# The prologue of a pooling and sparse-attention decoder step: quarters, group by group, keys by halves, and half of the key rows issued by GpSimd

## The reference

```python
hn = _rmsnorm(h, norms_l[0])
ext = concatenate([buf, hn], axis=1)              # buf: 15 older normed inputs (zeros for the prompt)
# group g of 512 channels: mean over the last w = 2, 4, 8 or 16 positions, less the input itself
s = c[:, POOL_BUF+1 : POOL_BUF+1+S] - c[:, POOL_BUF+1-w : POOL_BUF+1-w+S]      # c: running sum of ext
cnt = jnp.minimum(w, pos + 1)
mix = s / cnt - xf[:, POOL_BUF:]
mix = einsum('bsgc,gcd->bsgd', mix, w_pool_l) * scale_l       # a 512 x 512 matrix for each group
h = h + _rmsnorm(mix, norms_l[1]);  then a SwiGLU feed-forward of width 5632
# _compress of the past rows of each sample, keys and values (c = 0, 1), 16 pages of 128 rows each
first  = einsum('bnjche,cjef->bnchf', sub + pe[:16], cmp_w1[:, :16])
second = einsum('bnjche,cjef->bnchf', sub + pe[16:], cmp_w1[:, 16:])
hid = gelu(first[:, :-1] + second[:, 1:] + cmp_b1);  out = hid @ cmp_w2
```

## Time and profile before

| | us |
|---|---|
| median of three runs (range) | 2597.3 (2594.82 to 2601.64) |
| profiled execution, its own time | 2593.98 |
| span of the profile | 2592.4 |
| TensorE busy | 2528.8 (98%) |
| VectorE, ScalarE, GpSimd busy | 1212.3, 912.9, 291.1 |
| mean granted TensorE clock | 0.994 |

### The profile page before, as it was taken

How to read it: one execution, slowest core, us unless ns; L and a number is a source line. 1 busy time by engine, 2 the same in 40 slices (tenths; PEclk the granted TensorE clock), 3 DMA queues, 4 the chain that set the end, 5 groups by cost and what they waited for, 6 DMA issues and landing times.

```text
span 2592.4 us, 44035 instructions
## 1 busy us (share of the span) xinstructions
PE 2528.8 (98%) x17340; PEld 2476.0 (96%) x17340; DVE 1212.3 (47%) x1372; ACT 912.9 (35%) x1130; POOL 291.1 (11%) x324
## 2 busy tenths in 40 slices
PE   8799999999999999999999999999999999999997
PEld 6699999999999999999998789899999999999997
DVE  6654444444444444553434744744444444444444
ACT  3354323323332333442324643633333223323332
POOL 2430000000000001310001321300000000000012
PEclk9899999999999999999999999999999999999999
DMA  6524444444444444445545455344444444344443
GB/s 254 179 98 146 152 162 149 151 149 158 149 154 157 155 146 156 136 154 175 163 154 202 164 167 171 114 146 152 156 160 146 154 154 154 136 162 160 148 152 128
DMA packets 88809, 403.36 MB, mean 156 GB/s; under 512 B 13244, under 2 KB 23884, under 8 KB 58930
## 3 DMA queue, kind: packets, MB, share of 16 engines
q1 hardware_dynamic: 78674, 382.72, 43.5%
q0 software_dynamic: 6160, 12.60, 1.5%
q10 hardware_dynamic: 3920, 7.34, 0.8%
HBM read 394.88 MB, written 19.02 MB: 160 GB/s over the span
## 4 chain that ended last, share of the span: by engine, by line
PE 87%; DVE 6%; ACT 3%; issue 1%; SPq 1%; POOL 1%; DMA 1%; DVEq 0%; ACTq 0%
PE ps L1296 27%; PE ps L1297 27%; PE ps L1298 27%; ACT w_hi L479 1%; DVE w_lo L751 1%; PE ps L1387 1%; PE ps L1548 1%; PE ps L1474 1%; DVE winB L858 1%; DVE winA L858 1%; ACT y L587 0%; ACT x_hi L505 0%; SPq L361 0%; PE ps L1545 0%; POOL sc L1261 0%
## 5 line engine op out<-in xcount | busy, mean ns | idle before, releaser
L1296 PE MATMUL ps<-x_hi,w_hi 128*128 128x320 f32 x3536 | 1094.8, 310 | 5.9 <-DVE sg L922 2.4
L1297 PE MATMUL ps<-x_lo,w_hi 128*128 128x320 f32 x3536 | 1092.9, 309 | 0.0
L1298 PE MATMUL ps<-x_hi,w_lo 128*128 128x320 f32 x3536 | 1092.9, 309 | 0.0
L751 DVE TENSOR_TENSOR w_lo<-w_raw,w_hi 128x2048 fp32r<-128x2048 f32 (+1 forms) x364 | 748.9, 2058 | 651.8 <-ACT w_hi L479 651.8
L479 ACT CAST w_hi<-w_raw 128x2048 fp32r<-128x2048 f32 (+1 forms) x364 | 623.0, 1712 | 532.3 <-PE ps L1298 477.7
L1296 PEld LDWEIGHTS ps<-x_hi,w_hi 128*128 128x128 f32 x3536 | 664.1, 188 | 8.1 <-DVE sg L922 3.0
L1297 PEld LDWEIGHTS ps<-x_lo,w_hi 128*128 128x128 f32 x3536 | 664.0, 188 | 0.4 <-issue 0.2
L1298 PEld LDWEIGHTS ps<-x_hi,w_lo 128*128 128x128 f32 x3536 | 664.0, 188 | 0.0
L1296 PE MATMUL ps<-hid_hi,w_hi 128*128 128x320 f32 x1408 | 435.1, 309 | 0.0
L1297 PE MATMUL ps<-hid_lo,w_hi 128*128 128x320 f32 x1408 | 435.1, 309 | 0.0
L1298 PE MATMUL ps<-hid_hi,w_lo 128*128 128x320 f32 x1408 | 435.1, 309 | 0.0
(11 more groups left out here) (234 smaller groups left out, 1509.7 us busy)
## 6 DMA issues: line engine op xcount, KB each, us to landing
w_raw<-w_in_dram SPq DMA_DIRECT2D x176, 1024.0 KB, 4.9
w_raw<-w_out_dram SPq DMA_DIRECT2D x128, 704.0 KB, 4.0
w_raw<-w_kv_dram SPq DMA_DIRECT2D x24, 1024.0 KB, 6.6
w_raw<-w_q_dram SPq DMA_DIRECT2D x17, 1024.0 KB, 4.9
w_raw<-w_o_dram SPq DMA_DIRECT2D x15, 1024.0 KB, 5.6
win_out_dram<-win_kv_dram POOLq DMA_DIRECT2D x8, 992.0 KB, 5.3
rowsK<-cmp_data_dram SPq DMA_DIRECT2D x16, 256.0 KB, 9.1
w_raw<-w_pool_dram SPq DMA_DIRECT2D x4, 1024.0 KB, 6.4
```

What stands on the lines that cost most here:

```text
L751: V.tensor_tensor(w_lo[:, slot, 0:width], src, w_hi[:, slot, 0:width].bitcast(F32), ALU.subtract).then_inc(lo_made, 1)
L1296: M(out, wh, xh[:, k, :], start=(k == 0), stop=False)
L1297: M(out, wh, xl[:, k, :], start=False, stop=False)
L1298: last = M(out, wl, xh[:, k, :], start=False, stop=(k == kt - 1))
```

## The change

- The square sums of x leave TensorE: x comes in quarters; ScalarE squares quarters 0 and 2, VectorE quarters 1 and 3, and VectorE adds them up to one tile, over which TensorE sums once (`x_sum`).
- `inputs(g)` and `window_sums(g)` alternate group by group, with the outgoing states copied by group. The adds skip positions that no sum needs and treat prompt and samples in two instructions; the product with the counts is done for the first w - 1 positions only, and the rest is folded into the subtraction as a constant factor.
- Key rows: pages 0 to 7 go through SyncE's queue to the lo slots' memory, pages 8 to 15 are issued by GpSimd from its own queue to the raw slots' memory. `w1K` comes in two parts and lies over y. The key compression of the first half goes in two pieces, and signals `cmp_half`.
- `w_pool[0]` and `w_pool[1]` go through `w_rawX`, over x_hi and x_lo. Their splits stand between the window sums.
- The state outputs are issued after all four groups, before the third `x_lo`. ScalarE takes pool tiles 0 to 7 out of PSUM, VectorE 8 to 15.
- Both biases become products with the weights loaded and one moving column. The value bias now stands between the pool tiles and the value compression; the second copy of `w1V` and the transposing products are gone. 20 value positions stand ahead of `acc_sum`, and 44 behind it.
- SyncE issues `w_pool[3]` before `mix_made`, and the first two feed-forward panels after eight value pages.

```diff
...
+    rowsK = (at("rowsK0", "LO", [P, NP_ALL // 2, CS, 32], off=0), at("rowsK1", "RAW", [P, NP_ALL // 2, CS, 32], off=0))
+    w1K = at("w1K", "Y", [P, CB, P], off=0)
+    sq_all = at("sq_all", "X", [P, 4, GC * NT], off=0)
+    w_rawX = at("w_rawX", "X", [P, PW], off=KT // 2 * NT * 4)
...
+    winA = at("winA", "Z", [P, GC, EXT], off=0)
     winB = at("winB", "Z", [P, GC, EXT])
+    inv = at("inv", "Z", [P, NG, CS])
...
+        for i in range(4):
+            sp.dma_start(h[:, i * GC:(i + 1) * GC, :], x[:, i * GC:(i + 1) * GC, :]).then_inc(x_in[i], 16)
...
-        sp.dma_start(w1K[:, :, :], cmp_w1[0]).then_inc(cmpK_in[0], 16)
+        sp.dma_start(w1K[:, 0:CS, :], cmp_w1[0, :, 0:CS, :]).then_inc(w1K_in[0], 16)
         sp.wait_ge(pages_in, 16)
...
+        half = NP_ALL // 2
+        for p in range(half):
+            sp.dma_start(rowsK[0][:, p, :, :], cmp_data[0, page(p)]).then_inc(cmpK_in[0], 16)
+        sp.dma_start(stS[:, :, :, :], st[:, :, :, :]).then_inc(st_in, 16)
+        sp.dma_start(w1K[:, CS:CB, :], cmp_w1[0, :, CS:CB, :]).then_inc(w1K_in[1], 16)
+        sp.dma_start(inv[:, :, :], consts[:, C_INV:C_RV].rearrange("p (g t) -> p g t", g=NG)[:, :, 0:CS]).then_inc(inv_in, 16)
+        sp.wait_ge(stat_made, 1)
+        sp.dma_start(w_rawX[:, :], w_pool[0]).then_inc(raw_in[0], 16)
...
+        sp.wait_ge(lo_made, 1)
+        sp.dma_start(w_rawX[:, :], w_pool[1]).then_inc(raw_in[1], 16)
...
         sp.wait_ge(cmp_sum, 1)
-        panel(0, 0, w_pool[0], PW)
-        panel(1, 0, w_pool[1], PW)
+        panel(2, 0, w_pool[2], PW)
+        panel(3, 0, w_pool[3], PW)
         sp.wait_ge(mix_made, NG)
         sp.dma_start(w1V[:, :, :], cmp_w1[1]).then_inc(w1V_in, 16)
-        panel(2, 0, w_pool[2], PW)
         sp.wait_ge(mix_ready, NG)
         sp.wait_ge(states_out, 32)
         for p in range(NP_ALL):
...
+            if p == half:
+                across(P_FFN0, w_in0, 0)
+                across(P_FFN0, w_in0, 1)
+            sp.dma_start(rowsV[:, p, :, :], cmp_data[1, page(p)]).then_inc(cmpV_in[p // half], 16)
+        ffn(P_FFN0, w_in0, w_out0, 2)
+        for s in range(GC):
...
+        for q in (0, 2):
+            act.wait_ge(x_in[q], 16)
+            nc.scalar.square(sq_all[:, q, :], h[:, q * GC:(q + 1) * GC, :].rearrange("p c t -> p (c t)")).then_inc(sqx_made, 1)
...
+        def save_states(g):
+            c = slice(g * GC, (g + 1) * GC)
+            act.wait_ge(ext_made, g + 1)
+            nc.scalar.copy(stP[:, c, :], ext[:, c, SEQ:EXT_P])
+            nc.scalar.copy(stS[:, c, :, :], ext_s[:, c, :, DS:EXT_B]).then_inc(ext_saved, 1)
+        def mix_high(g):
             act.wait_ge(mix_made, g + 1)
             for dst, src in zip(by_tokens(x_hi, g), by_positions(ext, g)):
                 last = nc.scalar.copy(dst, src)
             last.then_inc(mixhi_made, 1)
+        def pool_tile(n):
+            act.wait_ge(tile_made, n + 1)
+            A(y[:, n, :], ps[:, n % 2, 0:NT], ACT.Copy, scale=gn[:, G_POOL, n:n + 1]).then_inc(bank_read[n % 2], 1)
+        save_states(0)
+        mix_high(0)
+        save_states(1)
+        hi_split(0, 0, src=w_rawX[:, :])
+        mix_high(1)
+        save_states(2)
+        hi_split(1, 0, src=w_rawX[:, :])
+        act.wait_ge(lo_made, 2)
+        mix_high(2)
+        pool_tile(0)
+        pool_tile(1)
+        save_states(3)
+        pool_tile(2)
+        pool_tile(3)
+        hi_split(2, 0)
+        for n in range(GC, 2 * GC - 1):
+            pool_tile(n)
+        mix_high(3)
+        pool_tile(2 * GC - 1)
+        hi_split(3, 0)
         def pool_ready(i):
...
+            if i == 12:
+                hi_split(P_FFN0, 0)
             act.wait_ge(bank_read[i % 2], i // 2 + 1)
         squares(1, y, pool_ready)
+        gelu(0, 0, hcS[:, 0, :])
+        sqrt_table()
...
+        for q in (1, 3):
+            dve.wait_ge(x_in[q], 16)
+            hq = h[:, q * GC:(q + 1) * GC, :].rearrange("p c t -> p (c t)")
+            link(V.tensor_tensor(sq_all[:, q, :], hq, hq, ALU.mult))
+            dve.wait_ge(sqx_made, q // 2 + 1)
+            link(V.tensor_tensor(sq_all[:, q - 1, :], sq_all[:, q - 1, :], sq_all[:, q, :], ALU.add))
+        link(V.tensor_tensor(sq_all[:, 1, :], sq_all[:, 0, :], sq_all[:, 2, :], ALU.add))
+        link(V.tensor_tensor(sq_all[:, 3, 0:2 * NT], sq_all[:, 1, 0:2 * NT], sq_all[:, 1, 2 * NT:4 * NT], ALU.add))
+        V.tensor_tensor(acc[:, :], sq_all[:, 3, 0:NT], sq_all[:, 3, NT:2 * NT], ALU.add).then_inc(x_sum, 1)
...
         def window_sums(g):
...
+            w = 2 ** (g + 1)
+            src, bufs = ext[:, g * GC:(g + 1) * GC, :], (winA, winB)
+            if g == 0:
+                dve.wait_ge(st_set, 1)
+                dve.wait_ge(inv_in, 16)
+            else:
                 dve.wait_ge(mix_made, g)
             for n in range(g + 1):
...
+                d, dst = 2 ** n, bufs[n % 2]
+                lo = BUF - (w - 2 * d)
+                (sp_, ss_), (dp_, ds_) = blocks(src), blocks(dst)
+                V.tensor_tensor(dp_[:, :, lo:EXT_P], sp_[:, :, lo:EXT_P], sp_[:, :, lo - d:EXT_P - d], ALU.add)
+                link(V.tensor_tensor(ds_[:, :, :, lo:EXT_B], ss_[:, :, :, lo:EXT_B], ss_[:, :, :, lo - d:EXT_B - d], ALU.add))
+                src = dst
+            (total, total_s), (x_, x_s) = by_positions(src, g), by_positions(ext, g)
+            first = total[:, :, 0:w - 1]
+            V.scalar_tensor_tensor(out=first, in0=first, scalar=float(w), in1=rep(inv[:, g, 0:w - 1], GC),
+                                   op0=ALU.mult, op1=ALU.mult)
+            full = rep(inv[:, g, CS - 1:CS].broadcast_to([P, DB * DS]), GC).rearrange("p c (b j) -> p c b j", b=DB)
+            link(V.tensor_tensor(total_s, total_s, full, ALU.mult))
+            dve.wait_ge(ext_saved, g + 1)
+            V.scalar_tensor_tensor(out=x_, in0=total, scalar=1.0 / w, in1=x_, op0=ALU.mult, op1=ALU.subtract)
+            V.tensor_tensor(x_s, total_s, x_s, ALU.subtract).then_inc(mix_made, 1)
...
+        inputs(0)
+        window_sums(0)
+        inputs(1)
+        window_sums(1)
+        dve.wait_ge(cmp_half, 1)
+        lo_split(0, 0, src=w_rawX[:, :])
+        inputs(2)
+        window_sums(2)
+        lo_split(1, 0, src=w_rawX[:, :])
+        inputs(3)
+        window_sums(3)
+        lo_split(2, 0)
+        for n in range(2 * GC, KT):
+            dve.wait_ge(tile_made, n + 1)
+            V.tensor_scalar(y[:, n, :], ps[:, n % 2, 0:NT], gn[:, G_POOL, n:n + 1], None,
+                            ALU.mult).then_inc(bank_read[n % 2], 1)
+            if n % GC == 0:
+                lo_split(n // GC + 1, 0)
+        def hidden_bias(c, col):
+            dve.wait_ge(b1_sum, c + 1)
+            V.tensor_tensor(b1e[:, c:c + 1], b1[:, c:c + 1], col, ALU.add).then_inc(b1_made, 1)
+        dve.wait_ge(const_in, 16 * 5)
+        hidden_bias(0, ps[:, 4, 0:1])
         cmp_join(0, 2, DB * NKV, True)
...
+        hidden_bias(1, ps[:, 0, 0:1])
+        dve.wait_ge(b1_made, 2)
...
+        half = NP_ALL // 2
+        pool.wait_ge(pages_in, 16)
+        for p in range(half):
+            n = pool.value_load(pgs[0:1, half + p:half + p + 1], min_val=0, max_val=cmp_data.shape[1] - 1)
+            pool.dma_start(rowsK[1][:, p, :, :], cmp_data[0, n]).then_inc(cmpK_in[1], 16)
         for g in range(NG):
             if g == 2:
+                pool.wait_ge(ext_saved, NG)
+                pool.dma_start(pool_p_out[:, :, :], stP[:, :, :]).then_inc(states_out, 16)
+                pool.dma_start(pool_s_out[:, :, :, :], stS[:, :, :, :]).then_inc(states_out, 16)
                 pool.wait_ge(states_out, 32)
...
+        def pos_bias(out, c, w1, lo, hi):
+            for j in range(lo, hi):
+                last = M(out, w1[:, j, :], pos[:, c, j:j + 1], start=(j == 0), stop=(j == CB - 1))
             return last
         pe.wait_ge(set_made, 1)
...
+        pe.wait_ge(w1K_in[0], 16)
+        pos_bias(ps[:, 4, 0:1], 0, w1K, 0, CS)
+        pe.wait_ge(x_sum, 1)
+        M(ps[:, STAT, 0:NT], ones[:, :], acc[:, :], start=True, stop=True).then_inc(stat_made, 1)
+        pe.wait_ge(cmpK_in[0], 16 * (NP_ALL // 2))
+        for j in range(CS):
+            compress(2, w1K, rowsK[0], 0, j)
+        pe.wait_ge(w1K_in[1], 16)
+        pos_bias(ps[:, 4, 0:1], 0, w1K, CS, CB).then_inc(b1_sum, 1)
+        for j in range(CS, CB):
+            last = compress(2, w1K, rowsK[0], 0, j)
+        last.then_inc(cmp_half, 1)
+        pe.wait_ge(cmpK_in[1], 16 * (NP_ALL // 2))
+        for j in range(CB):
+            last = compress(2, w1K, rowsK[1], 1, j)
         last.then_inc(cmp_sum, 1)
...
+        pe.wait_ge(w1V_in, 16)
+        pe.wait_ge(bank_read[0], KT // 2)
+        pos_bias(ps[:, 0, 0:1], 1, w1V, 0, CB).then_inc(b1_sum, 1)
+        def values(half, lo, hi):
+            n = NP_ALL // 2
+            pe.wait_ge(cmpV_in[half], 16 * n)
+            for j in range(lo, hi):
+                last = compress(5, w1V, rowsV[:, half * n:(half + 1) * n, :, :], half, j)
+            return last
```

(40 more changed lines are left out.)

136 lines of the change are left out of this document (27 added, 109 removed).

## The result

The kernel after takes 2604.5 us (median of 8 runs, 2598.0 to 2610.7), the kernel before 2596.0 (8 runs, 2594.5 to 2601.6). The ratio is 1.0032, 95% interval 1.0023 to 1.0042: 8.5 us slower, just over the 0.3% (7.8 us) that the prediction set for a difference. The forecast was 2596, in a range of 2588 to 2603, and "no change". The profiled execution took 2608.72, its span is 2607.1.

The account below looks back on a forecast made before the run. TensorE, busy 98% of the span, bounds the kernel; only the first feed-forward group's start moves. Panel split gains 10.2, value bias costs 7.1, clock 2.2: 0.9 us earlier, 2593.1 profiled, 2596 against all runs, range 2588 to 2603.

Parts of the forecast that it names:

- `inv` at 28.8: At the start, DMA engines full: `inv` lands at 28.8 us behind GpSimd's pages, and the first window sum starts at 29.
- r at 24: Root and reciprocal of x's square sums ready at about 24 us, against 23.8 before; not deciding, since `inv` is later.
- VectorE's stretch of 44.9: VectorE's window sums, inputs, splits and contention with `x_lo` take 44.9 us, so the last group is mixed at 73.9.
- `cmp_half` at 41: TensorE finishes the first half of the key compression at 41.1 us at full clock; `lo_split(0)` wants it at about 43.
- Rival B: Key compression by halves stays at 1.2 GHz, `cmp_half` comes at 58.6: 14.7 us slower, 2611; chance 0.09.
- rival C: Front of the kernel: lock contention, slower strided adds and `x_lo` of 6.5 make it 5 us late, 2600; chance 0.11.
- `x_lo` of 5.8: GpSimd's `x_lo` of the last group, beside one split, takes 5.8 us; ready at 81.1, against 81.62.
- What TensorE pays: Before the first feed-forward group: 7.1 us for the value bias now on the path, 2.2 us for the clock.
- the text's 4.4 us at half speed: After TensorE's idle time ahead of the last pool tile, some 4.4 us run at half speed: 2.2 us lost.
- 7.1 at half clock is 14: Upper bound for the value bias between pool tiles and value compression: 14 us at half clock, against the 7.1 taken.
- The forecast's own sign: Start of the first feed-forward group: net 0.9 us earlier, from 10.2 gained less 7.1 and 2.2.
- A: Rival: GpSimd's pages don't delay `inv` and the value bias costs 1.8 us: 11.5 us earlier, 2585; chance in full 0.15.

Follow-up runs that it names:

- e4: Kernel after with the second eight key pages issued by SyncE behind `inv`, none by GpSimd: 2597.8 us, 1.0007 of the kernel before.
- e6: Kernel after with TensorE's sum of squares first and the whole key bias behind the key compression: 2605.7 us, 1.0031 of the kernel before.
- e3: Kernel after with one of the 32 positions in the value bias, 31 products left out: 2588.9 us, 0.9973 of the kernel before.
- e8: Kernel before with only SyncE's order changed, `w_pool[3]` ahead of the value pages, first feed-forward panels after eight: 2591.5 us, ratio 0.9985.
- e1: Kernel after with the value bias moved ahead of the last pool tile, where TensorE idles: 2591.3 us, 0.9979 of the kernel before.
- e9: Kernel after with the value bias ahead of the last pool tile and all key rows issued by SyncE: 2583.0 us, 0.9959 of the kernel before.
- e2: Kernel after with 38 unread products of 128 moving columns ahead of the last pool tile: 2600.4 us, 1.0014 of the kernel before.
- e7: Kernel after with the edits of e1, e4 and e6 together: 2583.8 us, 0.9953 of the kernel before.
- e10: Edits of e9, but value bias ahead of pool tile 12, plus 20 unread 128-column products ahead of the last tile: 2590.2 us, ratio 0.9977.
- e5: Kernel after with the value bias replaced by 32 products, same weights, 128 moving columns of ones: 2596.3 us, 0.9998 of the kernel before.

## Why the prediction was wrong, step by step

- **`inv` at 28.8**: 16.21 + 13.3 = 29.5. Right, and right that GpSimd's pages stand ahead of it: without them, in e4, it lands at 24.2, near the text's lower end of 23.5.
- **r at 24**: 29.8. Two waits were missed. VectorE's first square waited until 14.02 for the gains, 80 KB queued behind x, and TensorE stood in the key bias when the sum was ready. VectorE also makes five passes over 1280 elements, not four (two squares and three adds, 1.49 each). "Nothing that decides" was wrong: the first window add began at 32.33, not 29, and of these 3.3 us `inv` explains 0.7; moving the sum alone gives 2.6 (e6).
- **VectorE's stretch of 44.9**: 45.6. Right. The contention came as forecast, though in another form: a product of 0.48 us took 2.40 beside `x_lo` (37.71), and an add 3.26 instead of 1.23 (71.57).
- **`cmp_half` at 41**: 46.53, since TensorE started 3.4 us late and took 8.98 us for the first 32 records, not 6.9; VectorE waited 0.39. Rival B (58.6) did not happen. Of rival C nothing happened either: the three meetings with `x_lo` cost 7.3 us in all (forecast 6.9), and the pieces of 256 elements took what their count says, 0.42. That its 2600 lies nearer to the measured time than the forecast is chance.
- **`x_lo` of 5.8**: 3.46, so 2.3 of the 3.3 + 0.7 us came back, which is luck: one error against another. Panel issued at 92.14 (forecast 90.6), landing 7.70, last tile at 104.59 instead of 102.9: **1.7 us late**.
- **What TensorE pays**: this is the step that failed. Forecast were 7.1 for the bias and 2.2 for the clock, 9.3; measured 17.7: 13.45 for the bias, 1.5 for the half-speed last tile (3.57 against 2.03) and 2.7 for the positions behind it. **8.4 us.** The price at full clock was right (32 records of the key bias took 3.47 us at 1.00, so 64 would take 6.9), and so was the clock term taken alone: in e3, without the bias, tile and positions lose 2.5, though the text's 4.4 us at half speed are more than the 3.4 of its row. What failed is that the two were added, as if the clock would come back under whatever work followed, though the text had the bound, 7.1 at half clock is 14. In e3 the bias's removal gives 14.6 back.

1.7 and 8.4 make the 10.1 us between 143.7 and 153.80. The mechanisms named were the right ones; the size of the bias was wrong, because the earlier trace rows showed the clock returning under matmuls of 320 columns and the earlier trace rows showed a bias of 128 columns, and neither shows what one column does. The forecast's own sign, 0.9 us earlier, hung on that term. No rival had it: A took the bias as cheaper, none as dearer, and with 14 instead of 7.1 the forecast would have been 2603. (In the sum of C, 5 us on 2596 are 2601, not 2600.)

Of the parts of the change, the runs price these at the group: SyncE's order gains 4.35 (in the kernel before, e8), the value bias behind the tiles costs 13.6 to 14.6 (e1, e3), GpSimd's queue 6.5 (e4), the key bias ahead of the sum 2.6 at the first add and nothing at the end (e6). With the two losses out, e9 has its group 11.6 us before that of the kernel before. SyncE's order alone gives 4.35 of that; the other 7 come from it together with the rest of the change, and no run takes that apart. Not tried was the kernel before with the new window sums alone, so their share, and that of the squares, stays open.

## What to carry to other kernels

- A product with one moving column was no cheaper than one with 128: 0.108 us a record here at full clock, against 0.11 for 128 columns. And after an idle gap all 64 records ran at half clock. Put such products where TensorE waits anyway; don't put them between a gap and dense work.
- Read a cost off a row only if its shape is that of the new operation; where clock and cost are two terms, ask whether the new work itself would bring the clock back.
- When the DMA engines are full, a second issuing queue changes what lands first. Count what is needed first, small loads too, and don't let an engine wait for a load that its next instructions do not use.
- A gain early in the chain is kept only if every engine's order lets it through; in e6 ScalarE's did not.

## What the runs showed of the hardware

- 64 records of one moving column and 128 weight columns take 13.45 us at granted clock 0.50 (0.210 each); the 32 at 35.87 take 3.47 us on the chain (0.108 each) at 1.00. In these runs the clock neither came back under such records (13.45 us without it, in after, e4 and e6) nor held: it fell from 1.00 to 0.50 during them in e1, e2, e7, e9 and e10. Under 64 records of 128 columns in the same place it came back (e5, 8.36 us).
- Behind the shorter key bias, 32 records, the clock differed from run to run: in e4 and e10 it fell to 0.50 in the key compression (e4 from 35 to 37.5 us), whose last 96 records took 22.65 us; in after and e9 it stayed at 1.00 and they took 20.97. In e1, e2, e3 and e5, whose programs are that of after up to there, it fell too, and VectorE waited 0.8 to 1.4 us for `cmp_half` instead of 0.39. So a single trace's start times behind this point are good to about 1 us.
- 40 records of 128 moving columns took 4.46 us on the chain at 1.00 (e10, 0.11 each): the same as with one column.
- In the first key bias, 18.82 to 25.8 us, 32 such records took 6.96 us, 0.217 each, as long as at half clock, while the view gives the granted clock as 1.00. TensorE had done nothing before. The key compression behind it begins slowly as well: 32 records in 8.98 us, the next 32 in 7.03, and counted by the microsecond four are under way up to 31 us and six from there on, while the view says 1.00 throughout. The durations speak for half clock until about 31 us; the view does not show it.
- A small load did not overtake: 80 KB of gains issued at 3.53 landed 10.5 us later, behind 2.6 MB of x and beside GpSimd's pages (e4, without these: VectorE released at 10.94, 3.1 earlier).
- A GpSimd page costs it 1.13 us, 0.54 of it the issue, much the same as SyncE's page (8.09 us for eight).
- VectorE's instructions that met GpSimd's `x_lo`: a product of 256 elements took 2.40 us instead of 0.48 (37.71, `x_lo` from 37.49), an add of 1024 took 3.26 instead of 1.23 (71.57, `x_lo` from 71.54).
